# Two transformer blocks in fp32: the order of work at the second norm, and eight weight pieces summed by VectorE instead of TensorE

## The reference

```
c_act = silu(c);  mod = c_act @ w_ada + b_ada          # (2048) @ (2048 x 12288)
sh1, sc1, gt1, sh2, sc2, gt2 = split(mod, 6)
h    = rms_norm(x, g_norm1) * (1 + sc1) + sh1
proj = h @ w_in                                         # q, k, v, two latents, k_pe
mix  = [differential attention | latent attention] @ w_out
x    = x + gt1 * mix
h2   = rms_norm(x, g_norm2) * (1 + sc2) + sh2
x    = x + gt2 * ((silu(h2 @ w_gate) * (h2 @ w_up)) @ w_down)
```

## Time and profile before

| | us |
|---|---|
| median of 3 runs | 2419.07 |
| profiled execution, whole | 2417.83 |
| its span, first to last instruction | 2416.1 |
| TensorE busy | 2319.9 |
| GpSimd busy | 1298.9 |
| ScalarE busy | 1030.5 |
| VectorE busy | 893.0 |

### The profile page before, as it was taken

The page is one execution under the profiler, slowest core; times in us unless marked ns, Lnnn a source line. Parts: engine busy times, 40 slices in busy tenths (PEclk is TensorE's granted clock), DMA queues, the critical chain, the costliest instruction groups (busy, mean ns, idle before and its releaser), DMA issues.

```text
span 2416.1 us, 29835 instructions
## 1 busy us (share of the span) xinstructions
PE 2319.9 (96%) x10764; PEld 1852.5 (77%) x10764; DVE 893.0 (37%) x1358; ACT 1030.5 (43%) x1275; POOL 1298.9 (54%) x622
## 2 busy tenths in 40 slices
PE   6899978979999999999999999999999999999997
PEld 3566645868888888888887887778888888888876
DVE  4354477861222211122244997521111111111265
ACT  3233355343344444444444443444444444444444
POOL 1100030007888888888881000068888888888800
PEclk9999999999999999999999999999999999999999
DMA  9989886745666666666656564666666656666554
GB/s 392 415 308 358 328 333 214 268 150 174 189 189 189 190 190 191 191 189 189 189 188 202 174 183 141 189 190 191 190 191 191 189 189 188 189 191 191 189 176 139
DMA packets 131275, 514.02 MB, mean 213 GB/s; under 512 B 14464, under 2 KB 20224, under 8 KB 118272
## 3 DMA queue, kind: packets, MB, share of 16 engines
q1 hardware_dynamic: 121408, 445.44, 57.6%
q0 software_dynamic: 9216, 67.11, 7.0%
q10 hardware_dynamic: 576, 0.47, 0.1%
HBM read 510.86 MB, written 2.10 MB: 212 GB/s over the span
## 4 chain that ended last, share of the span: by engine, by line
PE 78%; DVE 3%; ACT 1%; issue 1%; DVEq 0%; ACTq 0%
PE ps L1900 76%; PE ps L1803 1%; DVE w_lo L1344 1%; PE ps L1867 1%; DVE fm_lo L1319 0%; ACT fm_hi L666 0%; DVE gate L1598 0%; ACT w_hi L647 0%; DVE short L1081 0%; PE ps L1692 0%; PE ps L1714 0%; PE ps L1941 0%; ACT fm_hi L668 0%; DVE rstd L1279 0%; DVE x L1232 0%
## 5 line engine op out<-in xcount | busy, mean ns | idle before, releaser
L929 POOL TENSOR_TENSOR w_lo<-raw,w_hi 128x1024 fp32r<-128x1024 f32 x518 | 1241.1, 2396 | 502.4 <-ACT w_hi L647 502.4
L647 ACT ACTIVATE w_hi<-raw 128x1024 fp32r<-128x1024 f32 x766 | 809.2, 1058 | 1223.8 <-PE ps L1900 1182.6
L1900 PE MATMUL ps<-w_hi,fm_hi 128*128 128x512 f32 x2176 | 855.3, 393 | 16.1 <-DVE w_lo L1344 7.1
L1900 PE MATMUL ps<-w_hi,fm_lo 128*128 128x512 f32 x2176 | 847.4, 389 | 0.0
L1900 PE MATMUL ps<-w_lo,fm_hi 128*128 128x512 f32 x2176 | 847.3, 389 | 0.0
L1900 PEld LDWEIGHTS ps<-w_hi,fm_hi 128*128 128x128 f32 x2176 | 410.2, 188 | 125.4 <-issue 30.8
L1900 PEld LDWEIGHTS ps<-w_lo,fm_hi 128*128 128x128 f32 x2176 | 410.1, 188 | 85.5
L1900 PEld LDWEIGHTS ps<-w_hi,fm_lo 128*128 128x128 f32 x2176 | 410.1, 188 | 82.5 <-issue 0.2
L1344 DVE TENSOR_TENSOR w_lo<-raw,w_hi 128x1024 fp32r<-128x1024 f32 (+1 forms) x248 | 300.2, 1219 | 216.1 <-ACT w_hi L647 212.2
L1900 PE MATMUL ps<-w_hi,hid_hi 128*128 128x512 f32 x640 | 249.2, 389 | 0.0
L1900 PE MATMUL ps<-w_lo,hid_hi 128*128 128x512 f32 x640 | 249.0, 389 | 0.0
(11 more groups left out here) (281 smaller groups left out, 1409.8 us busy)
## 6 DMA issues: line engine op xcount, KB each, us to landing
raw<-in_w_gate SPq DMA_DIRECT2D x176, 512.0 KB, 3.5
raw<-in_w_up SPq DMA_DIRECT2D x176, 512.0 KB, 3.5
raw<-in_w_down SPq DMA_DIRECT2D x176, 512.0 KB, 3.5
ada_raw<-in_w_ada POOLq DMA_DIRECT2D x64, 1024.0 KB, 9.9
raw<-in_w_in SPq DMA_DIRECT2D x120, 512.0 KB, 3.8
raw<-in_w_out SPq DMA_DIRECT2D x64, 512.0 KB, 3.6
ada_raw<-in_w_ada SPq DMA_DIRECT2D x16, 1024.0 KB, 7.8
ada_raw<-in_w_gate SPq DMA_DIRECT2D x16, 1024.0 KB, 5.1
```

Source lines behind the costliest of these rows:

```text
L647: act.activation(w_hi[:, hi_slot, :, 0:width], raw[:, slot, :, 0:width], ACT.Copy).then_inc(hi_ready, 1)
L929: pool.tensor_tensor(w_lo[:, slot, :, 0:width], raw[:, slot, :, 0:width], w_hi[:, hi_slot, :, 0:width], ALU.subtract).then_inc(lo_ready, 1)
L1900: last = pe.matmul(banks[t][:, 0:width], a, b, start=kt == 0 and k == 0, stop=kt == kts - 1 and k == 2)
```

## The change

Two edits. In the input projection the pieces 33, 35, ... 47 of w_ada (`FOLDED`) go to VectorE, which adds each, times its column of silu(c), into `folded` (`fold`, after `rest(p)` and any copy at p = 26, 29, ... 47). `folded` lies where token half 0 of `y` lay. TensorE keeps the even pieces, now behind in1(p) with p % 3 == 0, and adds `folded` over the partitions behind in1(48) with four matmuls (`ada_fold`). The loads of GpSimd wait for `ada_folded` where the slot held such a piece. Turn and modulation of the group come one piece later. At the second norm VectorE does `rest` of the first piece before the norm and the others between the operand's banks; ScalarE scales two quarters, writes banks 0 to 3, scales the other two, makes three splits and then writes banks 4 to 7; TensorE turns banks 0 and 1, multiplies tiles 0 and 1, turns 2 and 3, multiplies tiles 2 to 5, and goes on as before.

```diff
--- before.py
+++ after.py
@@ -42,6 +42,14 @@
 ADA_PIECES = ADA_FIRST[-1]
 ADA_BANK = 7
 G_SHIFT2, G_GATE = 8, 10
+
+
+FOLDED = range(ADA_FIRST[G_SHIFT2] + 1, ADA_FIRST[G_SHIFT2 + 1], 2)
+
+
+def ada_steps(n):
+
+    return n - sum(k < n for k in FOLDED) + (n >= ADA_FIRST[G_SHIFT2 + 1])
 GATE2_RING = ADA - 1
 
 
@@ -192,6 +200,7 @@
         fm_t = at("fm_t", 84, [P, KT, S])
         gate = at("gate", 100, [P, D])
         c_wide = at("c_wide", 100, [P, KT, 32])
+        folded = at("folded", 16, [P, D])
 
         ident = at("ident", 108, [P, P])
         ones = at("ones", 108.5, [P, P])
...
@@ -613,7 +622,7 @@
                 act.activation(dst[:, :, :].rearrange("p k t -> p (k t)"), ps[:, bank:bank + 2, :].rearrange("p b t -> p (b t)"), ACT.Copy)\
                    .then_inc(hid_hi_ready, 1)
 
-            splits(f + AHEAD + 1, f + UP + AHEAD)
+            splits(f + AHEAD + 1 if done else f + 2 * AHEAD, f + UP + AHEAD)
             if done:
                 act.wait_ge(rstd_ready, 4)
             gate_tanh(0, f + 8)
@@ -688,11 +697,9 @@
                     if u == 2 and late:
                         splits(p + 4 * unit_pieces + AHEAD, p + 4 * unit_pieces + AHEAD + LATE)
 
-            def scale_x(n):
-                act.wait_ge(rstd_ready, n)
-                for q in range(4):
-                    act.activation(y[:, 0, q * NW:(q + 1) * NW], x[:, 0, q * NW:(q + 1) * NW], ACT.Copy,
-                                   scale=rstd[:, 0:1]).then_inc(y_scaled, 1)
+            def scale_second(q):
+                act.activation(y[:, 0, q * NW:(q + 1) * NW], x[:, 0, q * NW:(q + 1) * NW], ACT.Copy,
+                               scale=rstd[:, 0:1]).then_inc(y_scaled, 1)
 
             act_ffn_env = (act, split, splits, split_body)
 
...
@@ -746,13 +753,13 @@
             part_splits(24, 32 + AHEAD)
             operand_hi(cq_hi, col_b[:, 64:68], 2, AUX["cq"])
             operand_hi(ckv_hi, col_b[:, 68:70], 1, AUX["ckv"])
-            part_splits(32 + AHEAD, 48 + AHEAD)
+            part_splits(32 + AHEAD, 49 + AHEAD)
             copy_rows(G_SHIFT2, mod_rows[:, 0, :])
 
             act.wait_ge(unit_read, 6)
             for t in range(TT):
                 act.activation(y[:, t, :], qkv[:, t, 0:2048], ACT.Square).then_inc(squares, 1)
-            part_splits(48 + AHEAD, 64 + AHEAD)
+            part_splits(49 + AHEAD, 64 + AHEAD)
             act.wait_ge(unit_read, 8)
 
             following = 64 + AHEAD
@@ -851,9 +858,13 @@
                 for t in range(TT):
                     last = act.activation(y[:, t, cols], x[:, t, cols], ACT.Square, accum_out=x_sq[:, 4 * t + u:4 * t + u + 1])
                 last.then_inc(sumsq_act, 1)
-            scale_x(2)
+            act.wait_ge(rstd_ready, 2)
+            scale_second(0)
+            scale_second(1)
             operand_hi(fm_hi, gain2, 4, AUX["h2"], shift=shift2)
-            splits(FIRST["ffn1"] + AHEAD, FIRST["ffn1"] + AHEAD + 1)
+            scale_second(2)
+            scale_second(3)
+            splits(FIRST["ffn1"] + AHEAD, FIRST["ffn1"] + 2 * AHEAD)
             operand_hi(fm_hi, gain2, 8, AUX["h2"], 4, shift2)
             act_ffn(act_ffn_env, "ffn1", 0, operand_while)
             act_block2(act_ffn_env, operand_hi, squares_x, operand_while)
@@ -940,8 +951,10 @@
                         rest(i * body + p, p % RAW, p % SPLIT)
 
             def ada(n):
-                if n >= ADA:
-                    pool.wait_ge(ada_used, n - ADA + 1)
+                if n - ADA in FOLDED:
+                    pool.wait_ge(ada_folded, FOLDED.index(n - ADA) + 1)
+                elif n >= ADA:
+                    pool.wait_ge(ada_used, ada_steps(n - ADA + 1))
                 pool.dma_start(ada_raw[:, n % ADA, :], io["w_ada"][n]).then_inc(ada_landed[n % ADA], 16)
 
             for n in range(ADA):
@@ -1451,6 +1464,19 @@
             link(dve.tensor_scalar(lam[:, 0:1], lam[:, 0:1], -LAMBDA_INIT, None, ALU.add))
 
 
+            def fold(k):
+
+                n = FOLDED[k]
+                scale = c_act[:, n - ADA_FIRST[G_SHIFT2]:n - ADA_FIRST[G_SHIFT2] + 1]
+                dve.wait_ge(ada_landed[n % ADA], 16 * (n // ADA + 1))
+                if k == 0:
+                    dve.wait_ge(aux_drained, 9)
+                    dve.tensor_scalar(folded[:, :], ada_raw[:, n % ADA, :], scale, None, ALU.mult).then_inc(ada_folded, 1)
+                else:
+                    dve.wait_ge(ada_folded, k)
+                    dve.scalar_tensor_tensor(folded[:, :], ada_raw[:, n % ADA, :], scale, folded[:, :], ALU.mult, ALU.add)\
+                       .then_inc(ada_folded, 1)
+
             def latents():
 
                 for t in range(TT):
@@ -1498,7 +1524,9 @@
                 for r in range(8):
                     if p == in1_end(r) + AHEAD - 1:
                         in1_evacuate(r)
-                if p == 50:
+                if 26 <= p < 50 and p % 3 == 2:
+                    fold((p - 26) // 3)
+                if p == 51:
                     modulation(0, shift2, col_a[:, 80:96], gain2, col_a[:, 96:112], col_a[:, 64:80])
                 if p == 53:
                     dve.wait_ge(unit_read, 6)
...
@@ -1655,14 +1683,19 @@
                     last = dve.tensor_tensor(x[:, t, u * NW:(u + 1) * NW], x[:, t, u * NW:(u + 1) * NW], evac2[:, t, :], ALU.add)
                 last.then_inc(x_ready, 1)
                 dve.wait_ge(x_ready, u + 1)
+            rest(FIRST["ffn1"])
             norm_x()
-            for k in range(3):
+            h2_lo(0)
+            for k in range(1, AHEAD):
                 rest(FIRST["ffn1"] + k)
-            for k in range(3):
                 h2_lo(k)
-            for k in range(3, UP):
+            h2_lo(AHEAD)
+            for k in range(AHEAD, 2 * AHEAD):
+                rest(FIRST["ffn1"] + k)
+            for k in range(AHEAD + 1, UP):
                 h2_lo(k)
-                rest(FIRST["ffn1"] + k)
+                if k >= UP - 2:
+                    rest(FIRST["ffn1"] + k)
             add_gate(gate2, gate2_bias, 32)
             dve_ffn(env, "ffn1", 0, col_a[:, 112:128])
             dve_block2(env)
@@ -1782,7 +1815,10 @@
             def gate_first():
                 banks, early = (ps[:, 0, :], ps[:, 1, :]), range(LATE_TILES if done else 6)
                 pe.wait_ge(unit_read, units)
-                product(fm_hi, fm_lo, KT, f, banks, NW, f, operand_after, part=early)
+                if not done:
+                    product(fm_hi, fm_lo, KT, f, banks, NW, f, operand_after, part=range(0, 2))
+                    env["turn_y"](2, 2, 4)
+                product(fm_hi, fm_lo, KT, f, banks, NW, f, operand_after, part=early if done else range(2, 6))
                 if done:
                     env["turn_x"](4, 3)
                     pe.wait_ge(p_landed, 16)
@@ -1922,7 +1958,15 @@
                 for q in range(4):
                     kt = 4 * m + q if group < EIGHTHS else m
                     last = pe.matmul(ps[32 * q:32 * q + 32, ADA_BANK, :], c_wide[:, kt, :],
-                                     ada_raw[:, n % ADA, q * NW:(q + 1) * NW], start=m == 0, stop=m == last_m)
+                                     ada_raw[:, n % ADA, q * NW:(q + 1) * NW], start=m == 0, stop=m == last_m and group != G_SHIFT2)
+                last.then_inc(ada_used, 1)
+
+            def ada_fold():
+
+                pe.wait_ge(ada_folded, len(FOLDED))
+                for q in range(4):
+                    last = pe.matmul(ps[32 * q:32 * q + 32, ADA_BANK, :], ones[:, 0:32], folded[:, q * NW:(q + 1) * NW],
+                                     start=False, stop=True)
                 last.then_inc(ada_used, 1)
 
             def turn_columns(group):
@@ -1994,16 +2038,19 @@
                 if j == 0:
                     pe.wait_ge(unit_read, r - 1)
                 in1(p)
-                if p % 3 == 2:
+                if p == 48:
+                    ada_fold()
+                elif p % 3 == 0:
                     ada(n)
-                    ada(n + 1)
+                    if n + 1 not in FOLDED:
+                        ada(n + 1)
                     n += 2
                 if p == in1_end(3) - 1:
                     pe.wait_ge(lat_ready, 1)
                     pe.wait_ge(unit_read, 3)
                     turn_tiles(2, lambda kt, t: lat[:, t, kt * P:(kt + 1) * P])
                     turn_tiles(1, lambda kt, t: lat[:, t, NW + kt * P:NW + (kt + 1) * P])
-                if p == 49:
+                if p == 50:
                     turn_columns(G_SHIFT2)
             while n < ADA_FIRST[G_SHIFT2 + 1] + 10:
                 ada(n)
@@ -2114,7 +2161,7 @@
                 unit(15 + u, fm_hi, fm_lo, KT, FIRST["out1"] + UP * u, operand_after=OPERANDS["mix1"] if u == 0 else None)
                 if u == 0:
                     spread_gate(gate_rows)
-            turn_y(2, 0, 4)
+            turn_y(2, 0, 2)
             pe_ffn(pe_env, "ffn1", 0, N_OUT1, AUX["in2"], OPERANDS["h2"])
             pe_block2(pe_env, counts)
```

(12 more changed lines are left out.)

## The result

The changed kernel takes 2404.51 us, the median of 5 runs (2403.40 to 2407.35); the kernel before 2419.07 (2417.15 to 2420.66). The ratio is 0.9943, 95% interval 0.9932 to 0.9955: 11 to 16.5 us less. I forecast 2408.2 and a range that began at 2405.5. The profiled execution took 2404.13 us, 13.7 less than the one of before.

The account below looks back on a forecast made before the run. TensorE, busy 96% of the span, was taken to bound the kernel. The input projection's 5.66 us plus the second norm's 5.2 made 10.9, taking 2419.07 to 2408.2 us; range 2405.5 to 2415 for 8 in 10.

Parts of the forecast that it names:

- Part one, the price of the pieces: Input projection: eight cycles each lose a 0.86 us w_ada piece, one 1.22 us event is added; saves 5.66 us.
- Part one, its two ends: Input projection, first cycle and added event behind in1(48): priced like steady cycles; whole saving bounded at 4.8 to 6.0 us.
- the first sum: VectorE's sum before rest(27), called the tight place: zero cost by 0.2 us, at most 1.29 us without that cover.
- the event at p = 48: Added event behind in1(48): no row for it, between 0.86 and 2.08 us, taken as 1.22 us.
- the gap before 142.12: Input projection, start of the stretch: some 0.2 us the change may also take in, left out of the sum.
- Transfers: Input projection: shorter cycle needs 390 GB/s; cost taken as zero, with 1.1 us kept as possible loss.
- the rival: Input projection: transfers bind, cycle stays near 10.28 us, part one brings nothing, time 2413.9 us; chance 0.13.
- Part two, the start: Second norm: TensorE's first product starts at 522.45 instead of 524.83, gain 2.35 us, bounds 0 to 2.9.
- Part two, the stall: Second norm: second wait of 2.11 us and its slow clock go, about 2.8 us of the 5.2 gain.
- the second stall stays: Second norm: a thin margin fails, split chain 2 us late, only the start gained, time 2411.1 us; chance 0.17.
- Sum: Both places together: 5.66 + 5.2 = 10.9 us, giving 2408.2 us against the median of 2419.07.

Follow-up runs that it names:

- e5: Changed kernel with TensorE's single w_ada pieces back behind p % 3 == 2 (26 to 47), sums unmoved; in1(24) to the latents' products took 134.24 us.
- e6: Changed kernel with VectorE's sums one piece later, at p % 3 == 0 (27 to 48); in1(24) to the latents' products took 133.01 us.
- e12: Changed kernel with TensorE's even pieces of group 8 after the first on 128 columns instead of 512, leaving work out; cycle 8.75 us, one execution 2403.20 us.
- e2: Kernel before with only the second-norm edit (six hunks); median 2414.23 us of 11, ratio 0.9982.
- e4: Changed kernel run again, unchanged; median 2406.49 us of 5, ratio 0.9948.
- e8: Changed kernel run once more, unchanged; median 2405.24 us of 5, ratio 0.9942.
- e11: Changed kernel with ScalarE's splits of 110 and 111 and VectorE's rest of them back behind banks 4 to 7; ratio 0.9965 against before.
- e1: Kernel before with all of the diff except the second-norm hunks; median 2413.23 us of 9, ratio 0.9975.
- e9: Changed kernel with later sums, latents' norm cut in three on VectorE, and in1(24) writing banks 0 and 1; median 2402.72 us of 5, ratio 0.9934.

## Why the prediction was off, point by point

- **Part one, the price of the pieces.** Right: cycle 9.39 (forecast 9.42), sums of 2.35 and 1.28 us, and no wait for a landing. The tile's view of the changed kernel from 136 to 225 us has the longest at 11.4 us, against the 15.6 allowed:

```profile
DMA to landing us min/median/max: 7.1/8.3/11.4
```

- **Part one, its two ends: the term that was mis-sized.** This is the step that failed: 5.66 us, with an upper bound of 6.0, where every trace of the changed kernel shows 6.5. I had priced all eight cycles and the event at p = 48 by the steady cycle. In the first cycle I charged the single event behind in1(24) at 1.22 and the first sum at zero "by 0.2 us". in1(26) waits for VectorE's latents in any case, so the event is hidden (e5), and the first sum costs a wait of 0.5 and the restart, 0.8 in all (e6): in1(24) to in1(27) gained 1.25 us where I had 0.86. The next seven cycles gained 6.15 (I had 6.02), and behind in1(48) the kernel lost 0.86 (I had 1.22): the event there costs some 1.05 us, by my estimate. A piece behind a pair takes 2.89 us and not 2.72; this 0.17 went with the pair before in1(48), and as the last pair now ends the stretch, another 0.17 falls behind the cut. In all 6.5, in three traces of either kernel. About 0.4 of the excess is the first cycle, 0.1 the steady ones and 0.4 the end. The row for the first cycle was the gap before 142.12, which I saw and left out: it marked an in1(26) bound by VectorE.
- **Transfers.** No cost, as taken; the rival falls with e12. By the Trainium skill's limit of about 358 GB/s (DMA: Bandwidth & Descriptors, "Where 436 GB/s comes from") e12's cycle could not have been under 10.25 us. Its 401 GB/s over 60 us say otherwise on this core. The section works the figure out as half of a stack's rate, for two cores; this kernel runs on one, and no run here shows what two would get.
- **Part two, the start.** 4.19 us from turn to product instead of 6.16: 1.97, forecast 2.35. ScalarE reached the first bank at 1.13 us after the turn began and not 0.8, as it waits 0.61 for the turn, and VectorE then 1.34 for ScalarE.
- **Part two, the stall.** The stall of 2.11 us went, as forecast, in all nine traces. The size, 5.1 from turn to sums in the first pair against my 5.2, agrees by luck of the clock: e2, e4 and e8 gained 3.6 to 3.9. I had taken 4.41 us for the first twelve matmuls, from one row; they took 4.23 in the first trace and 5.26 in e4. And the split into 2.35 and 2.8 was wrong: e11 shows that the start alone brings 0.1 at most. The rival "the second stall stays" was worth about 0 at this place, not 2.35.
- **Sum.** 6.5 + 5.1 less 0.2 behind the latents is 11.4 us for the first pair of traces, cut by cut; with e4 and e8 it is some 10. By the means of three traces each the two places gave 6.5 + 4.2 - 0.2 = 10.5, near my 10.9 only because one term was too low and the other too high. The rest of the first pair's 13.7 (1.35 and 1.57, less 0.6) is the same code in another phase of loads and clock: no row of my sum had it, and I allowed too little for it below. Part one's missing 0.85 alone would have put the forecast at about 2407.4, inside the range; it took this luck as well to leave it. The medians lie 12 to 14.5 apart in the three pairs, the traced executions 11.5 on average. The traced executions of before (2417.83, 2417.83, 2416.87) lie below its mean of 2418.58 over 25, and the clock of its executions over 2420 is mostly 0.984 (0.983 to 0.987) against 0.987 to 0.989 in those traced, so before seems to lose more to the clock in executions that were not traced. What the medians show beyond the two places, 2 to 4 us, stays open: no trace of such an execution of before was taken, only e1's with the old norm (clock 0.984), which lost 2.5 us at the norm.

## What to carry to other kernels

When work is taken out of the engine that bounds a stretch, look for the one place in it where another engine's chain ends last, even by 0.2 us: work put there is free, and work put on that other engine there is not. A slow clock or a wait in such a place is no loss that can be won back alone; moving one half of a chain (e11) turns it into another wait. When the expected gain is near the spread of one kernel's executions, cut several traces at the same marks and compare the cuts rather than the totals. One trace of each kernel is not enough even then: the cut at the second norm moved by 1.4 us between traces of the changed kernel.

## What the runs showed of the hardware

The clock behind a wait differs between executions of the same code. At u1 all traces wait 1.84 us; in before the sixth matmul behind it took 0.63 us (1.2 GHz), in after 0.39 (2.4 GHz), and that is the 1.57 us between u1 and u2.

```profile
1270.57 0.63 PE L1900 MATMUL ps<-w_lo,fm_hi 128*128 128x512 f32 x1
```

```profile
1257.33 0.39 PE L1936 MATMUL ps<-w_lo,fm_hi 128*128 128x512 f32 x1
```

Of 14 traces four kept the clock there (18.0 us from u1 to u2, not 19.6), the first of after, e1, e6 and e9. So the same wait of 1.84 us was followed by 1.2 GHz in ten traces and by the full clock in four. At the second norm it was alike: behind the waits of 2.1 us at the stalls the clock fell in the three traces of before, and at the first stall of e1 and both of e11 it stayed.
